# Last layer norm: gain before the inverse root, and one operation for scale and offset in the last two blocks

## What is computed

```python
h = _layernorm(DN_ALPHA * h + f, ln2_g[l], ln2_b[l])

def _layernorm(x, g, b):
    mu = jnp.mean(xf, axis=-1, keepdims=True)
    xc = xf - mu
    var = jnp.mean(xc * xc, axis=-1, keepdims=True)
    y = xc * lax.rsqrt(var + LN_EPS) * g + b
```

## Time and profile before

| | us |
|---|---|
| runs, median of 3 | 1847.8 (1846.37 to 1848.26) |
| the profiled execution | 1843.17 |
| its span in the trace | 1841.4 |
| around the span (1843.17 - 1841.4) | 1.8 |

### The profile page before, as it was taken

One profiled execution on the slowest core, in us unless ns is written; L12 is line 12 of the kernel. 1 busy time (PEld: TensorE's weight loads), 2 busy tenths in 40 slices (PEclk: granted clock), 3 DMA queues, 4 the chain that ended last, 5 costly groups with the idle time before them and its releaser, 6 DMA issues.

```text
span 1841.4 us, 23075 instructions
## 1 busy us (share of the span) xinstructions
PE 1781.6 (97%) x8596; PEld 1483.4 (81%) x8596; DVE 909.4 (49%) x1515; ACT 719.3 (39%) x1295; POOL 914.2 (50%) x718
## 2 busy tenths in 40 slices
PE   8999999999999999999989999999999999999996
PEld 6788887888898777888867888778888888788884
DVE  6213313444444485545455535765455544666446
ACT  6544333333433224545451113744444444211122
POOL 6887754211221642332413375876777766334343
PEclk9999999999999999999999999999999999999998
DMA  5434324214121568222334344132222322754422
GB/s 173 128 106 123 114 78 149 81 47 93 56 82 69 179 222 273 89 82 93 107 105 149 134 175 145 63 109 75 91 69 80 103 78 90 255 193 151 162 101 92
DMA packets 202525, 219.39 MB, mean 119 GB/s; under 512 B 22381, under 2 KB 145437, under 8 KB 202413
## 3 DMA queue, kind: packets, MB, share of 16 engines
q1 hardware_dynamic: 164350, 144.76, 25.1%
q10 hardware_dynamic: 38064, 73.15, 11.1%
HBM read 159.14 MB, written 58.74 MB: 118 GB/s over the span
## 4 chain that ended last, share of the span: by engine, by line
PE 81%; DVE 6%; DMA 4%; POOL 4%; ACT 2%; issue 2%; SPq 1%; ACTq 0%; DVEq 0%; POOLq 0%
PE psum_all L1055 23%; PE psum_all L1057 23%; PE psum_all L1056 23%; DMA ga_st<-d_sga 1%; PE psum_all L1392 1%; PE psum_all L1376 1%; PE psum_all L1393 1%; PE psum_all L1394 1%; DVE pT_lo L1576 1%; PE psum_all L1119 1%; PE psum_all L1123 1%; PE psum_all L1121 1%; POOL s_sb L993 1%; POOL w_lo L990 1%; PE psum_all L1364 1%
## 5 line engine op out<-in xcount | busy, mean ns | idle before, releaser
L928 POOL CAST w_hi<-w_raw 128x512 fp32r<-128x512 f32 (+4 forms) x104 | 91.5, 880 | 496.3 <-PE psum_all L1057 469.7
L930 POOL TENSOR_TENSOR w_lo<-w_raw,w_hi 128x512 fp32r<-128x512 f32 (+4 forms) x104 | 212.5, 2043 | 8.5
L1055 PE MATMUL psum_all<-xT_hi,w_hi 128*128 128x512 f32 (+1 forms) x456 | 181.0, 397 | 5.2 <-POOL w_lo L864 3.3
L1057 PE MATMUL psum_all<-xT_hi,w_lo 128*128 128x512 f32 (+1 forms) x456 | 178.1, 390 | 0.0
L1056 PE MATMUL psum_all<-xT_lo,w_hi 128*128 128x512 f32 (+1 forms) x456 | 177.6, 390 | 0.0
L1055 PE MATMUL psum_all<-t_hi,w_hi 128*128 128x512 f32 x352 | 138.0, 392 | 2.5 <-DVE psum_all L2190 2.2
L1056 PE MATMUL psum_all<-t_lo,w_hi 128*128 128x512 f32 x352 | 137.6, 391 | 0.0
L1057 PE MATMUL psum_all<-t_hi,w_lo 128*128 128x512 f32 x352 | 137.5, 391 | 0.0
L990 POOL TENSOR_TENSOR w_lo<-s_sb,w_hi 128x512 fp32r<-128x512 f32 x88 | 112.7, 1293 | 41.9 <-ACT w_hi L2780 41.9
L944 POOL TENSOR_SCALAR p_sb<-p_sb,small 128x128 f32<-128x128 f32 (+3 forms) x64 | 47.8, 748 | 171.4 <-DVE small L1954 171.3
L990 POOL TENSOR_TENSOR w_lo<-w_raw,w_hi 128x512 fp32r<-128x512 f32 x66 | 84.8, 1287 | 57.9 <-ACT w_hi L2780 57.8
(11 more groups left out here) (536 smaller groups left out, 4878.4 us busy)
## 6 DMA issues: line engine op xcount, KB each, us to landing
w_raw<-in_w_up_dram SPq DMA_DIRECT2D x44, 512.0 KB, 3.9
f_raw<-d_f SPq DMA_DIRECT2D x44, 512.0 KB, 3.4
w_raw<-in_w_in_dram SPq DMA_DIRECT2D x36, 512.0 KB, 4.6
d_f<-up_g SPq DMA_DIRECT2D x44, 256.0 KB, 3.7
w_raw<-in_w_down_dram SPq DMA_DIRECT2D x22, 512.0 KB, 4.5
w_raw<-in_w_out_dram SPq DMA_DIRECT2D x8, 1024.0 KB, 5.1
x_tok<-in_x_dram SPq DMA_DIRECT2D x8, 512.0 KB, 6.6
d_sga<-x_st ACTq DMA_DIRECT2D x16, 256.0 KB, 2.0
```

The lines of the kernel that those rows point to most:

```text
L928: wc.done(nc.gpsimd.tensor_copy(w_hi[b][:, w], src[:, w]))
L930: low = nc.gpsimd.tensor_tensor(w_lo[b][:, w], src[:, w], w_hi[b][:, w].bitcast(F32), ALU.subtract)
L1055: pe.matmul(out_ap, ah, bh, start=start and i == 0, stop=False, skip_group_check=more)
L1057: last = pe.matmul(out_ap, al, bh, start=False, stop=stop and i == len(terms) - 1, skip_group_check=more)
```

## The change

VectorE now does `(z - mean) * gain` of block t in one `scalar_tensor_tensor` (L2250 of the changed kernel, called `gained`) right after the variance of the same block, then the reciprocal (L2257, `inverse`). ScalarE only multiplies by the inverse root (L3009, `Copy` with one per-token factor), after both. GpSimd's addition of the offset (still L1043) is now released by ScalarE. For blocks 6 and 7 ScalarE does no wide pass: VectorE does `z * inverse root + offset` in one operation (L2253, `offset`).

```diff
@@ gpsimd
             for t in range(TT - 2):
-                pool.wait_ge(sm["ln2_g"], t + 1)
+                pool.wait_ge(sm["ln2_n"], t + 1)
                 nc.gpsimd.tensor_tensor(z_tok[:, t, :], z_tok[:, t, :], ln2_bt[:, :], ALU.add).then_inc(sm["ln2_ok"], 1)
@@ vector
+            def gained(t, c):
+                return V.scalar_tensor_tensor(z_tok[:, t, c], z_tok[:, t, c], mv2[:, t, 0:1], ln2_gt[:, c], ALU.subtract, ALU.mult)
+            def offset(t, c):
+                return V.scalar_tensor_tensor(z_tok[:, t, c], z_tok[:, t, c], lrs2[:, t, 1:2], ln2_bt[:, c], ALU.mult, ALU.add)
+            def inverse(t):
+                ve.wait_ge(sm["ln2_s"], t + 1)
+                V.reciprocal(lrs2[:, t, 1:2], lrs2[:, t, 0:1]).then_inc(sm["ln2_r"], 1)
             for t in range(TT):
                 ...
                 row_var(bst2, mv2, lrs2, t, sm["ln2_v"])
-                if t >= 1:
-                    ve.wait_ge(sm["ln2_n"], t)
-                    V.tensor_tensor(z_tok[:, t - 1, :], z_tok[:, t - 1, :], ln2_gt[:, :], ALU.mult).then_inc(sm["ln2_g"], 1)
-                row_scale(mv2, lrs2, t, sm["ln2_s"], sm["ln2_r"])
+                if t < TT - 1:
+                    gained(t, slice(0, D)).then_inc(sm["ln2_g"], 1)
+                    inverse(t)
             ve.wait_ge(sm["ln2_g"], TT - 1)
-            V.tensor_tensor(z_tok[:, TT - 2, :], z_tok[:, TT - 2, :], ln2_bt[:, :], ALU.add).then_inc(sm["ln2_g"], 1)
+            ve.wait_ge(sm["ln2_r"], TT - 1)
+            offset(TT - 2, slice(0, D)).then_inc(sm["ln2_end"], 1)
             for g in range(2):
-                c = slice(g * HALF, (g + 1) * HALF)
-                ve.wait_ge(sm["ln2_n"], TT + g)
-                vc.done(V.tensor_tensor(z_tok[:, TT - 1, c], z_tok[:, TT - 1, c], ln2_gt[:, c], ALU.mult))
-            for g in range(2):
-                c = slice(g * HALF, (g + 1) * HALF)
-                vc.wait(vc.n - 1 + g)
-                V.tensor_tensor(z_tok[:, TT - 1, c], z_tok[:, TT - 1, c], ln2_bt[:, c], ALU.add).then_inc(sm["ln2_end"], 1)
+                vc.done(gained(TT - 1, slice(g * HALF, (g + 1) * HALF)))
+                if g == 0:
+                    inverse(TT - 1)
+                    ve.wait_ge(sm["ln2_r"], TT)
+                vc.wait()
+                offset(TT - 1, slice(g * HALF, (g + 1) * HALF)).then_inc(sm["ln2_end"], 1)
@@ scalar
-                if t < TT - 1:
+                if t < TT - 2:
+                    ac.wait_ge(sm["ln2_g"], t + 1)
                     ac.wait_ge(sm["ln2_r"], t + 1)
-                    A.activation(z_tok[:, t, :], z_tok[:, t, :], ACT.Identity, bias=lrs2[:, t, 2:3], scale=lrs2[:, t, 1:2]).then_inc(sm["ln2_n"], 1)
+                    A.activation(z_tok[:, t, :], z_tok[:, t, :], ACT.Copy, scale=lrs2[:, t, 1:2]).then_inc(sm["ln2_n"], 1)
                 ...
-            ac.wait_ge(sm["ln2_r"], TT)
-            for g in range(2):
-                c = slice(g * HALF, (g + 1) * HALF)
-                A.activation(z_tok[:, TT - 1, c], z_tok[:, TT - 1, c], ACT.Identity, bias=lrs2[:, TT - 1, 2:3],
-                             scale=lrs2[:, TT - 1, 1:2]).then_inc(sm["ln2_n"], 1)
```

More of the change, by code:

```diff
@@ L839, in _ @@
                     f_load(q)
-            sp.wait_ge(sm["ln2_end"], 2)
+            sp.wait_ge(sm["ln2_end"], 3)
             sp.dma_start(out[0, (TT - 1) * P:, HALF:D], z_tok[:, TT - 1, HALF:D]).then_inc(sm["out_stored"], 16)
@@ L3010, in _ @@
                 else:
-                    ac.wait_ge(sm["ln2_g"], TT)
+                    ac.wait_ge(sm["ln2_end"], 1)
                 ac.dma_start(out[0, t * P:(t + 1) * P, :], z_tok[:, t, :]).then_inc(sm["out_stored"], 16)
-            ac.wait_ge(sm["ln2_end"], 1)
+            ac.wait_ge(sm["ln2_end"], 2)
             ac.dma_start(out[0, (TT - 1) * P:, 0:HALF], z_tok[:, TT - 1, 0:HALF]).then_inc(sm["out_stored"], 16)
```

## The result

The changed kernel takes 1856.04 us (median of 4 runs, 1854.37 to 1856.67) against 1847.43 (4 runs, 1846.37 to 1848.26): ratio 1.0045, 95% interval 1.0028 to 1.0063, that is 8.6 us slower. The profiled execution took 1856.67 us, with a span of 1854.9.

What follows compares the result with a forecast made beforehand. Bound: GpSimd's addition and VectorE's wide SBUF operation exclude each other. Block 7's turn +7.49 us (4.2 loop, 3.3 place), end -0.46: +7.0 on the median 1847.8 gives 1854.8 us, range 1851.5 to 1857.5 (8 in 10).

Steps and rivals of the forecast that it cites:

- The bound of a block: Blocks in the ending chain: GpSimd's addition and VectorE's wide operation take turns, 3.53 us summed, 3.56 in the trace.
- the kind of the new operation: VectorE's `gained`: two SBUF tiles, so it waits out GpSimd's addition and lasts some 3.05 us instead of 1.27.
- no standing still: Rival: `gained` doesn't wait for GpSimd; turns of 3.00 us, -3.5 us, 1844.3; chance 0.07.
- Block 0 earlier: Block 0's gain is applied earlier; first GpSimd addition 1810.82 to 1813.20, ending 1.92 us sooner than before.
- The loop: Per block, ScalarE's pass now stands between VectorE's and GpSimd's possessions: 4.78 us for 3.56, five loops, +6.1 us.
- The end: From block 7's turn to the span's end: 10.27 us against 10.73, set by crowded stores; 8.49 if stores don't limit.
- The saving of 0.46: The tail behind block 7's start: 10.27 us against 10.73 before, the stores limiting; 2.24 saved if they don't.
- The 1.42: Last stores: us around the full DMA stretch, taken from 2.10 MB moved in the kernel before and reused for 2.62 MB.
- Sum: Whole span: block 7's turn 7.49 us later, less 0.46 at the end, +7.0 us; 1854.8 us for the median.
- The 1850.2 forecast for the profiled execution: Profiled execution's 1843.17 us plus the forecast +7.0 us on the span.
- VectorE comes first: Rival: next block's `gained` gets in ahead of GpSimd's addition; 3.33 us per block, -1.8 us, 1846.0; chance 0.06.
- the margin: In every block GpSimd takes possession 0.41 us before VectorE's next `gained` is ready, so GpSimd is first.

Runs made afterwards that it cites:

- gain in PSUM: Changed kernel, but the gain for blocks 2 to 7 is read from PSUM, copied there by ScalarE; ratio to before 1.0002, stretch 33.77 us.
- only the end changed: Kernel before for blocks 0 to 5, blocks 6 and 7 as in the changed kernel; ratio to before 1.0006, stretch 35.19 us.
- without GpSimd's additions: Changed kernel with a 128x1 memset in place of GpSimd's six offset additions; one run, stretch 32.01 us against 43.33.
- SP's stores: Changed kernel with the stores of blocks 0 to 6 issued by SP's queue instead of ScalarE's; ratio to before 1.0036, stretch 40.91 us.
- next gained first: Changed kernel with GpSimd's addition of block t also waiting for VectorE's gained of block t + 1; ratio to before 1.0010, stretch 34.97 us.
- ScalarE later: Changed kernel with a 128x512 ScalarE copy into a dead buffer before each of its six wide passes; ratio to before 1.0009, stretch 33.29 us.
- before, gain in PSUM: Kernel before with the gain for blocks 1 to 6 read from PSUM, copied by ScalarE; ratio to before 0.9996, stretch 32.82 us.

## Why the prediction was right

- *The bound of a block and the kind of the new operation.* Right: `gained` beside GpSimd lasted 3.08 to 3.36 us (3.05 foreseen), each ending 1.08 us behind an addition, and 1.27 without one. By the "gain in PSUM" run this is shown, not only argued. The rival "no standing still" is out. The Trainium skill's "Advanced Engine Details and Errata", section "VectorE Performance Modes", names only two-port instructions as the ones that interfere; these runs show more, 3.08 to 3.36 us for an fp32 operation that takes 1.27 alone. The Trainium skill's "SBUF — State Buffer", section "SBUF: two separate sides", gives a VectorE operation with two SBUF inputs the same exclusive lock against a GpSimd operation that reads SBUF; these runs agree, with 3.15 us for the gain from SBUF and 1.27 for the gain from PSUM in one trace.
- *Block 0 earlier.* The first addition started 4.43 us behind block 0's product; 1810.82 - 1806.47 = 4.35 were foreseen.
- *The loop.* 4.78 foreseen, 4.87 measured. Too small were ScalarE's release, 0.10 for 0.03 (1824.42 to 1824.52), and by 0.01 to 0.02 GpSimd's addition (2.39 or 2.40 for 2.38). Block 4's pass starts 0.37 us behind its reciprocal (1834.12 to 1834.49) and makes one loop 5.10. Block 0's to block 7's addition: 32.38 against a forecast of 1838.16 - 1806.47 = 31.69.
- *The end.* The term mis-sized: 10.27 foreseen, 10.95 measured. VectorE's share was right (5.95 and 6.01), and so was what sets the end, the bunched stores. The full stretch of the DMA engines lasted from about 1846.6 to 1853.3 (a share of 0.29 from 1853 to 1854), 6.7 us where 6.51 were summed. But 0.8 us lay ahead of it, from the first issue at 1845.81, and 1.2 behind it, to the last landing at 1849.99 + 4.5 = 1854.5: 2.0 in all, where 1.42 were summed. The 1.42 was also read wrongly from before. From 1834.31 on its trace shows 2.24 MB moved, not 2.10, since a store issued at 1832.55 was still under way, so the DMA engines were busy when that bunch began; in the changed kernel they started from rest. The saving of 0.46 became a loss of 0.22.
- *Sum.* +7.0 foreseen, +8.4 in the traces, +8.6 in the medians; 1856.04 lies within 1851.5 to 1857.5. 0.7 us of the difference in the traces is the loop with its release, 0.7 the end; both terms were too small, nothing cancelled. The 1850.2 forecast for the profiled execution compares badly with 1856.67, since that execution reached the norm 5.1 us later than the one of before (1811.57 for 1806.47), which the sum could not know.
- *"VectorE comes first".* Not what happens in the changed kernel, but the switch is real: a shift of 0.53 us in ScalarE crosses the margin (0.41 computed, 0.34 in the trace: 1820.88 to 1821.22), and the foreseen pace of 3.33 us came out at 3.35.

## What to carry to other kernels

When a wide VectorE operation with two SBUF inputs is longer in some places than in others, look for a GpSimd row that ends a fixed time ahead of its end (1.08 us here, for 128x1024 in fp32). If both engines do such operations in a loop, count the time of either as one resource, and keep other engines' work out of the path between two holders; a wait that fixes the order (8.4 us of the stretch here) or one input moved to PSUM (9.6 us) can be worth more than any operation that is saved. Issue stores from a queue that has nothing to wait for: it was worth 2.4 us of the stretch here.

## What the hardware showed that was not expected

- In the changed kernel the issue of three stores of 512 KB on ScalarE's queue took 2.54 us and the next 1.20, where a single one takes 0.34. With the stores spread over time by SP every issue took 0.33 to 0.36. So the issues were long where several stores of the same queue were under way; why was not tested.
- With the stores bunched, the last landed 1.2 us after the DMA engines' full stretch was over in the changed kernel, and 0.5 us after it in the one with only the end changed; a lone store of 256 KB needed 2.0 us in all.
- ScalarE's pass of block 4 starts 0.37 to 0.39 us after the reciprocal instead of 0.10 in the changed kernel, in that without GpSimd's additions, in that with SP's stores, and in that with the next gained first. In the one with ScalarE later it is block 3's turn that has it. It is absent in the two changed kernels that have the copy to PSUM ahead of it. It isn't the store, which SP issues in one of them. The 0.28 us that VectorE stood in "before, gain in PSUM" may be the same thing or another. The cause stays open; it costs 0.27 us.
- A one-input-in-PSUM `scalar_tensor_tensor` of 128x1024 is as fast as the SBUF one, 1.27 us.
